# Latent attention: scores of two key blocks per step, the rotary products in the two row halves of the array

## The reference, cut to what matters

```python
    qa = jnp.concatenate([q_nope, q_rope], axis=-1)             # (B,S,8,128+64)
    ka = jnp.concatenate([k_nope, jnp.broadcast_to(k_rope[:, :, None, :], (B, S, A_HEADS, A_ROPE))], axis=-1)
    ha = causal_block_attention(qa, ka, v_a) * jax.nn.silu(a_z)

    # inside, per head, with scale = 1/sqrt(192)
    s = jnp.einsum('bhqd,bshd->bhqs', qi, k).astype(jnp.float32) * scale
    s = jnp.where(k_pos[None, :] <= q_pos[:, None], s, -jnp.inf)
    p = jax.nn.softmax(s, axis=-1)
    return jnp.einsum('bhqs,bshd->bqhd', p.astype(v.dtype), v)
```

## Time and profile before

| | us |
|---|---|
| median of 3 runs (2812.47 to 3058.36) | 2815.47 |
| the profiled execution, its own time | 2817.33 |
| its span on the slowest core (core 7) | 2816.1 |
| spans of the eight cores | 2789.0 to 2816.1 |
| attention stage, first L1295 to last L1325 | 1131.2 to 1591.4 |

### The profile page before, as it was taken

How to read it: one execution, slowest core, us unless ns; L and a number is a source line. 1 busy time by engine, 2 the same in 40 slices (tenths; PEclk the granted TensorE clock), 3 DMA queues, 4 the chain that set the end, 5 groups by cost and what they waited for, 6 DMA issues and landing times.

```text
span 2816.1 us, 42574 instructions; the slowest of 8 cores (2789.0 to 2816.1 us)
## 1 busy us (share of the span) xinstructions
PE 2698.2 (96%) x14245; PEld 1303.7 (46%) x14245; DVE 943.8 (34%) x1783; ACT 771.4 (27%) x1551; POOL 446.6 (16%) x643
## 2 busy tenths in 40 slices
PE   7999998998998999999999989999999999999998
PEld 4445444444454444455555444444444444444443
DVE  5356673364654433232223341111113211111123
ACT  5223321112444443444444441111112111111111
POOL 2101101131232221000000000332321122122111
PEclk9999999999999999999999999999999999999999
DMA  9648553254463664446325477557558744444453
GB/s 256 172 88 180 103 108 66 41 115 98 95 113 92 146 158 123 110 101 136 93 63 116 112 200 206 109 110 147 117 116 221 212 79 79 79 69 78 68 150 120
DMA packets 198678, 340.98 MB, mean 121 GB/s; under 512 B 47617, under 2 KB 142145, under 8 KB 191809
## 3 DMA queue, kind: packets, MB, share of 16 engines
q0 software_dynamic: 31392, 138.26, 29.3%
q1 hardware_dynamic: 167074, 200.01, 24.2%
HBM read 390.19 MB, written 86.28 MB: 169 GB/s over the span
## 4 chain that ended last, share of the span: by engine, by line
PE 84%; DMA 9%; DVE 3%; issue 2%; ACT 1%; SPq 1%; POOL 0%; DVEq 0%; ACTq 0%; POOLq 0%
PE bk L505 22%; PE bk L1485 20%; PE bk L493 14%; PE bk L1493 10%; PE bk L1664 7%; PE bk L1325 2%; PE bk L1295 2%; PE bk L1297 2%; DMA m_mv<-MV 1%; DMA m_cq<-CQT 1%; DMA m_hb<-wOUT 1%; DMA m_wgb<-wGB 1%; DMA ACC<-m_tmpc 1%; DMA m_w<-wA 1%; DMA HCT<-m_hcT 1%
## 5 line engine op out<-in xcount | busy, mean ns | idle before, releaser
L505 PE MATMUL bk<-m_w,m_hT 128*128 128x512 bf16 x3072 | 728.8, 381 | 16.7 <-DMA m_w<-wA 6.0
L1485 PE MATMUL bk<-m_hT,m_wgb 128*128 128x512 bf16 x3072 | 706.4, 380 | 4.2 <-ACT m_sg L1490 2.5
L1485 PEld LDWEIGHTS bk<-m_hT,m_wgb 128*128 128x128 bf16 x3072 | 299.1, 98 | 358.1 <-issue 7.6
L505 PEld LDWEIGHTS bk<-m_w,m_hT 128*128 128x128 bf16 x3072 | 296.3, 98 | 347.1 <-issue 30.5
L1493 PE MATMUL bk<-m_hb,m_wgb 128*128 128x512 bf16 x1536 | 368.0, 380 | 3.0 <-DVE m_tmpc L1498 2.6
L493 PE MATMUL bk<-m_hT,m_w 128*128 128x512 bf16 (+1 forms) x1600 | 359.4, 380 | 7.0 <-DVE m_t L862 6.3
L1498 DVE SCALAR_TENSOR_TENSOR m_tmpc<-m_sg,bk 128x512 f32<-128x512 f32 x160 | 110.0, 688 | 654.4 <-PE bk L1485 446.5
L1490 ACT ACTIVATE m_sg<-bk 128x512 f32<-128x512 f32 x192 | 114.7, 598 | 778.0 <-PE bk L1485 728.2
L493 PEld LDWEIGHTS bk<-m_hT,m_w 128*128 128x128 bf16 (+1 forms) x1600 | 156.7, 99 | 191.3 <-issue 13.1
L1300 ACT ACTIVATE m_Pa<-bk 128x512 bf16<-128x512 f32 (+1 forms) x320 | 169.0, 533 | 236.8 <-PE bk L1297 150.9
L1493 PEld LDWEIGHTS bk<-m_hb,m_wgb 128*128 128x128 bf16 x1536 | 149.5, 98 | 179.3 <-issue 5.6
(11 more groups left out here) (182 smaller groups left out, 2239.5 us busy)
## 6 DMA issues: line engine op xcount, KB each, us to landing
m_wgb<-wGB POOLq DMA_DIRECT2D x96, 768.0 KB, 7.8
m_w<-wA POOLq DMA_DIRECT2D x72, 512.0 KB, 12.6
m_xt<-x SPq DMA_DIRECT2D x16, 1024.0 KB, 12.1
m_xo<-x SPq DMA_DIRECT2D x16, 1024.0 KB, 10.8
out<-m_xo SPq DMA_DIRECT2D x15, 1024.0 KB, 4.3
m_w<-wMEM POOLq DMA_DIRECT2D x16, 512.0 KB, 18.2
ACC<-m_tmpc SPq DMA_DIRECT2D x32, 256.0 KB, 7.2
m_accl<-ACC SPq DMA_DIRECT2D x16, 512.0 KB, 5.1
```

The lines of the kernel that those rows point to most:

```text
L505: fw.op("pe", lambda e: e.matmul(bk[:, 0:ncols], lhsT=src(kc, tt * 128, 128), rhs=w[:, kc, 0:ncols], start=(kc == 0), stop=(kc == KC - 1)) ...
L1485: fw.op("pe", lambda e: e.matmul(gb[:, 0:512], lhsT=w[:, kc, :], rhs=mg_t["h0"][:, kc, tcs], start=(kc == 0), stop=(kc == 15)), reads=[w.r ...
```

## The change

Two key blocks (`2*kp`, `2*kp+1`) form one item, so there are 160. Their four score products are issued in the order plain, plain, rotary, rotary, into both banks of `s_banks`. The rotary tiles `kr` and `qr` hold their 64 rows twice, in partitions 0 to 63 and again in 64 to 127 (a second DMA each in place of the zeros). The rotary product of the even block takes the lower half of the rows as operands, that of the odd block the upper half. The loop now issues, for pair n: a waiting tail (if `kp == 1`), `scores(n+1)`, a yield, PV of pair n, a yield. The totals of `mix` and the sum of what `mla` yields are as before.

```diff
-            fw.op("dve", lambda e: e.memset(kr[64:128, :], 0.0), writes=[kr.r])
-            fw.dma("sp", kr[0:64, :], KRT_d, reads=[m_KRT], writes=[kr.r])
+            for half in (slice(0, 64), slice(64, 128)):
+                fw.dma("sp", kr[half, :], KRT_d, reads=[m_KRT], writes=[kr.r])
...
-            for qr in qrs:
-                fw.op("dve", lambda e: e.memset(qr[64:128, :], 0.0), writes=[qr.r])
...
-                fw.dma("sp", qrs[s][0:64, :], QRT_d[h * 64:(h + 1) * 64, :], reads=[m_QR], writes=[qrs[s].r])
+                for half in (slice(0, 64), slice(64, 128)):
+                    fw.dma("sp", qrs[s][half, :], QRT_d[h * 64:(h + 1) * 64, :], reads=[m_QR], writes=[qrs[s].r])
...
+                for kt, q_lo, ncols, bs, r_bs in both:
+                    fw.op("pe", lambda e: e.matmul(bs[:, 0:ncols], lhsT=kn[:, kt * 128:(kt + 1) * 128], rhs=qn[:, q_lo * 128:q_lo * 128 + ncols],
+                                                   start=True, stop=False), reads=[kn.r, qn.r], writes=[r_bs])
+                for kt, q_lo, ncols, bs, r_bs in both:
+                    half = slice(64 * (kt % 2), 64 * (kt % 2) + 64)
+                    fw.op("pe", lambda e: e.matmul(bs[:, 0:ncols], lhsT=kr[half, kt * 128:(kt + 1) * 128], rhs=qr[half, q_lo * 128:q_lo * 128 + ncols],
+                                                   start=False, stop=True), reads=[kr.r, qr.r], writes=[r_bs])
...
+                if kp == 1 and tails:
+                    tails.pop(0)()
+                if n + 1 < len(items):
+                    scores(n + 1)
...
+                yield 1
+                for kt, P, q_lo in wait_P.pop(n):
+                    for qt in range(q_lo, 4 * qb + 4):
...
-                if n + 2 < len(items):
-                    scores(n + 2)
-                if kt == 2 and tails:
-                    tails.pop(0)()
```

More of the change, by code:

```diff
@@ L1282, in load_az @@
                        reads=[m_AZ[h // 4]], writes=[azs[s].r])
-            items = [(h, qb, kt) for h in range(8) for qb in range(4) for kt in range(4 * qb + 4)]
+            items = [(h, qb, kp) for h in range(8) for qb in range(4) for kp in range(2 * qb + 2)]
             wait_P = {}
             def scores(n):
-                h, qb, kt = items[n]
+                h, qb, kp = items[n]
                 qn, qr, kn = (x[h % 2] for x in (qns, qrs, kns))
[L1290 to L1304, removed]
@@ new lines, in scores @@
+                both = []
+                for kt in (2 * kp, 2 * kp + 1):
+                    q_lo = max(kt, 4 * qb)
+                    both.append((kt, q_lo, (4 * qb + 4 - q_lo) * 128) + s_banks())
+                for kt, q_lo, ncols, bs, r_bs in both:
+                    fw.op("pe", lambda e: e.matmul(bs[:, 0:ncols], lhsT=kn[:, kt * 128:(kt + 1) * 128], rhs=qn[:, q_lo * 128:q_lo * 128 + ncols],
+                                                   start=True, stop=False), reads=[kn.r, qn.r], writes=[r_bs])
@@ new lines, in scores @@
+                for kt, q_lo, ncols, bs, r_bs in both:
+                    half = slice(64 * (kt % 2), 64 * (kt % 2) + 64)
+                    fw.op("pe", lambda e: e.matmul(bs[:, 0:ncols], lhsT=kr[half, kt * 128:(kt + 1) * 128], rhs=qr[half, q_lo * 128:q_lo * 128 + ncols],
+                                                   start=False, stop=True), reads=[kr.r, qr.r], writes=[r_bs])
+                wait_P[n] = []
+                for kt, q_lo, ncols, bs, r_bs in both:
+                    P = nxt_P()
+                    fw.op("act", lambda e: e.activation(out=P[:, 0:ncols], in_=bs[:, 0:ncols], func=AF.Exp, scale=SC), reads=[r_bs], writes=[P.r])
+                    if kt >= 4 * qb:
+                        fw.op("dve", lambda e: e.tensor_tensor(out=P[:, 0:128], in0=P[:, 0:128], in1=maskb[:], op=ALU.mult),
+                              reads=[P.r, maskb.r], writes=[P.r])
+                    wait_P[n].append((kt, P, q_lo))
@@ L1314, in mla @@
             load_az(0)
-            for n in range(2):
-                scores(n)
-                yield 1
+            scores(0)
+            yield 2
             tails = []
-            for n, (h, qb, kt) in enumerate(items):
+            for n, (h, qb, kp) in enumerate(items):
                 vx, az = vxs[h % 2], azs[h % 2]
[L1321 to L1328, removed]
+                if kp == 1 and tails:
+                    tails.pop(0)()
+                if n + 1 < len(items):
+                    scores(n + 1)
+                if qb == 1 and kp == 0 and h + 1 < 8:
                     loads(h + 1)
                     load_az(h + 1)
-                if n + 2 < len(items):
-                    scores(n + 2)
-                if kt == 2 and tails:
-                    tails.pop(0)()
-                if kt < 4 * qb + 3:
+                yield 1
+                for kt, P, q_lo in wait_P.pop(n):
+                    for qt in range(q_lo, 4 * qb + 4):
+                        jj = qt - q_lo
+                        bo, r_bo = o_of(qt - 4 * qb)
+                        fw.op("pe", lambda e: e.matmul(bo, lhsT=P[:, jj * 128:(jj + 1) * 128], rhs=vx[:, kt, 0:129],
+                                                       start=(kt == 0), stop=(kt == qt)),
+                              reads=[P.r, vx.r], writes=[r_bo])
+                if kp < 2 * qb + 1:
                     yield 1
```

## The result

The changed kernel is slower by half a per cent: ratio of its times to those of before 1.0048, 95% interval 1.0029 to 1.0067, that is 13.5 us on 2814. The ratio goes by two of its four executions, 2829.65 us (the profiled one) and 2825.0, since in the other two (3323.93 and 2874.27) one die ran at a lower granted clock.

A forecast was written before the change was run, and what follows sets the result against it. TensorE, busy 96% of the slowest core's span, was taken as the bound. Columns -27.7, changes of rows +25.6 and waits -0.2 gave -2.3 us on 2815.5, about 2813 us; range 2785 to 2846.

The forecast's parts named there:

- the slow rivals: Attention stage: each change of rows empties TensorE, 2849 us (chance 0.16); halves run one after another, 2841 us (chance 0.12).
- DMA "at nothing": Loads of the rotary tiles: one more DMA per head, issued a head ahead, some 57 us, costs nothing.
- 7.5 us once: Loads of the rotary tiles: without the lead time, a late load would cost its 7.5 us to landing once.
- Changes of rows: TensorE around each rotary pair: to half rows and back 160 times at 0.16 us, +25.6 us.
- the slower rival: Around rotary pairs: each change empties TensorE, 0.38 us a pair, deciding from 0.17; 2849 us, chance 0.16.
- Columns side by side: Rotary products: both halves stream at once, so the shorter product of each pair is free, -27.7 us.
- o banks: PV's waits for the drained o banks: fall from 19.1 to 2.4 us, left at head changes.
- The tail's bank: Second plain product waits for the copy of the tail's transposes: 0.61 us at 31 tails, late copies 5, together 24 us.
- Two exponentials: Second plain product of the next pair needs both exponentials of this pair: about 1 us of waits.
- the rival with a worse chain of exponentials: ScalarE and VectorE: filler results ahead of exponentials cost 9 us, late copies 8 more; 2830 us, chance 0.08.
- Waits in all: TensorE's waits in the attention stage: 28.9 us after for 29.1 before, so -0.2 us.
- The signs named in advance: Changed trace: rotary starts within some 10 ns, first 0.30 us behind plain, about 31 copy waits, stage 445 to 475 us.

The follow-up runs named there:

- e1_own_wait: Changed kernel with the two halves of kr and of qr recorded apart, so the second DMA needn't wait; ratio to before 1.0007, stage 462.8 us.
- e2_full_height: Changed kernel, pairs and order kept, rotary products at full height with zeros again, one DMA each; ratio to before 0.9983, stage 456.8 us.
- e6_half_per_item: Kernel before with every single rotary product on rows 0 to 63 only, 320 changes there and back; ratio to before 1.0212, stage 516.9 us on six cores.
- e3_same_half: e1_own_wait with both rotary products in the lower half of the rows, nothing side by side; ratio to before 1.0101, stage 488.2 to 490.8 us.
- e4_tail_early: e1_own_wait with the tail's transposes and copy issued one yield earlier; ratio to before 0.9941, stage 447.0 to 447.4 us.

## Why the prediction was wrong, point by point

The forecast was a change of -2.3 us, 2813 us; measured are +8.4 us in the stage and +13.5 us in the ratio, some 2829 us. That lies inside the stated range of 2785 to 2846, but the range reached so far up for the slow rivals; the sum pointed the other way. Two of its terms failed, the DMA that was put at nothing and the changes of rows that were priced too low.

- **DMA "at nothing": wrong, 5.6 us (e1_own_wait).** This is the step that failed by its reasoning. I counted one more DMA per head, issued a head ahead. For the first head there is no head ahead, `kr`, loaded once at the start, is split too, and both halves write one record, so the second waits on SyncE's queue until the first has landed, with everything queued behind it. I had read the order of the queue (two issues in a row) and not what the second one waits for. My price for a late load, "7.5 us once", was near what core 2 lost, but not for its reason: 4.75 us of idling, and then 3.2 us by the clock, which I had not counted at all.
- **Changes of rows, +25.6 us: right in kind, 7.4 us too small.** I took 0.16 us a pair from the eight-row transposes; measured are 33.0 us, 0.21 a pair (e1_own_wait against e2_full_height; e6_half_per_item has the same price). It is this term that turns the halves from a small gain into a loss: above 0.17 us a pair, the point named in the slower rival, they cost more than they save. The slower rival took this side, but with 0.38 us a pair. The Trainium skill ("TensorEngine Tiling (Array Packing)", Key Properties) says that a change of tiling mode drains TensorE; the runs agree that each change delays the next matmul, by 0.10 us here, less than the 0.163 us that I had put on a full run-out.
- **Columns side by side, -27.7 us: right.** The distances between starts give 27.1 us; the 3 ns between the two starts, 0.5 us in all, are the difference. Against e3_same_half the stage shows 25.4, as 1.9 us go into longer waits.
- **o banks, 19.1 to 2.4 us: right,** 2.4 us measured (4 and 2 events, 1.4 us on record).
- **The tail's bank, 24 us: right in mechanism, close in size.** 31 waits as forecast, 26.3 us; moving the transposes took 15.8 us off the stage (e4_tail_early).
- **Two exponentials, 1 us: close.** No wait of L1295 for an exponential is left in the list, so the rival with a worse chain of exponentials falls.
- **Waits in all, -0.2 us: -3.4 by the gaps, -3.2 by the stage (e2_full_height).** The list of waits leaves out gaps shorter than the 0.163 us that a record hides; the timeline gives 33.1 us before where I had 29.1.

The errors add up to the miss, in the mean of the cores: 5.6 for the DMA and its clock, 7.4 for the changes of rows, 0.6 for the columns, -3.0 for the waits, together 10.6 us; from -2.3 to +8.4 it is 10.7. Without the DMA's wait the changed kernel would still have been no gain: e1_own_wait has +2.8 us in the stage, and its ratio of 1.0007 can't be told from 1.

The signs named in advance mostly came: the second rotary product 3 ns behind the first, the first 0.31 us behind the second plain product, 31 waits for the copy, the stage between 445 and 475 us. They were all signs of TensorE; none of them would have shown the wait on SyncE's queue.

**What stays open:** the ratio of the slowest core shows 13.5 us where the stage and the mean span show 8.4 and 8.5. In the profiled executions the slowest core before (core 7) has 1131.4 us ahead of the stage, 460.0 in it and 1224.7 behind it; the slowest one after (core 2) has 1126.0, 470.1 and 1232.6. So what the slowest core has beyond the stage lies behind it, 7.9 us, and there core 2 lost 16.1 us to stretches at a granted clock of 0.50 where core 7 lost 10.1. The kernel before has such stretches too (5 to 14 us lost behind the stage, by core), so which core gets most of them sets part of this time; whether the change has a share in it is not shown. It is open as well why only five of the eight cores of e3_same_half fell to 0.50 in the stage, though all eight have the same three waits of 1.7 us. Nor was it tried to group more than two blocks, which would halve the number of changes of rows: all eight PSUM banks are in use.

## What to carry to other kernels

Half-height matmuls side by side saved the shorter of two, 0.216 us for 512 columns, but entering and leaving the half rows cost 0.21 us, so one pair between full-height matmuls gained nothing here; price the changes before the columns. When a DMA is split in two on one tile, ask what record the second one writes: it may wait for the first to land and hold the whole queue. And when two banks are asked for at once, look for who else uses one of them: a tail moved by one yield was worth more here than the change itself.

## What the runs showed of the hardware that I had not expected

- A weight load for half rows is not issued ahead behind a full-height matmul, nor the other way round: at all 320 changes (changed kernel, core 2) and all 640 of e6_half_per_item (core 6) it starts 4 ns ahead of its matmul in the median, where a filler's load behind a filler starts 214 ns ahead. The matmul comes some 0.10 us late going in and coming out, with one load as with two, and the full-height matmul after that one is still 10 ns late.
- Two matmuls in different halves of the rows start 3 ns apart (median of 160 pairs, on each of the eight cores) and take 0.39 us together.
- An idle stretch of 4.6 us left TensorE at a granted clock of 0.50 for the next 6 us; the work of that time went at half rate. The same place without the idling stayed at 1.00 (e1_own_wait). In e3_same_half such a stretch followed a wait of 1.7 us, on five cores of eight, and cost another 1.7 us.
